# Two stacked blocks in split fp32: retention with its values first, rotary columns packed, and other places for the attention steps

## The chip, the cores and the metric

One core of one Trainium2 chip runs the kernel. The metric is the device time of one execution in microseconds (us). The kernel before takes 3192.93 us, the median of three runs (3192.46 to 3195.58).

## What is computed

Two networks of two layers each over 512 tokens of width 1024, one after the other, in float32.

Each layer of the first one ("mix") normalizes x, projects it and runs three attentions: differential attention (4 heads, "da"), latent attention (8 heads, "mla", two heads at a time) and sliding-window attention (8 heads, "sw", two at a time). Their gated outputs go through branch projections and an output projection; a gated embedding ("ple") follows. In latent attention a score is a 64-wide product plus a 32-wide rotary one:

```python
s = (jnp.einsum('bqhd,bkhd->bhqk', qn, kn)
     + jnp.einsum('bqhr,bkr->bhqk', qr, kr)) * scale
```

The second network has retention in its first layer: 4 heads with queries and keys 256 wide and values 512 wide, scores times a decay, no softmax, and then a normalization of the 512 outputs of a head to mean 0 and variance 1 (`mu`, `var`), times a gate. Its second layer has attention over three dilations (128, 512 and 2048 tokens), 16 heads, computed for two heads at a time in eight rounds. A convolutional feed-forward block follows each of the two.

## The kernel before

**Products.** All activations lie transposed, features in the partitions and the 512 tokens along the free axis. A linear product is a stream of steps; one step is a 128x128 piece of a weight against 128x512 of the activations, in three matmuls (L668 to L670: weight high part times activation high part, times low part, weight low part times high part). Eight steps (a tile) give 128 output columns when the inner dimension is 1024. `open` (L641) makes a tile wait until the bank of PSUM that it writes has been evicted. The weights come as a stream of chunks of eight steps through a ring of three buffers: SP loads a chunk, ScalarE casts the high part (L1145), GpSimd subtracts the low part (L535), and the matmuls use it.

**Order.** Each engine has its own program, written out by hand, and they meet at semaphores. `ORDER` (L70) lists for each of the 12 heads or pairs of heads of a layer which tiles TensorE computes beside the head's attention: gates, branches and the projections of the next head. `cuts` (L98) divides this work of head n into 12 equal parts. TensorE's loop over the four blocks of 128 queries (L843 on) puts three places into each block: after the first part `scores` of the next block, after the second `turn` (the transposes of the probabilities, L803), after the third `values` (probabilities times values, L823). The other engines follow the same cuts: VectorE takes the maxima of the scores, waits for the sums of ScalarE's exponentials, divides, and evicts the tiles in between (`beside`, L1885).

**Latent rotary columns.** The key's 32 rotary columns are projected twice, straight (`kr`, 8 steps) and with their halves swapped (`ks`, 8 steps), each with unused columns between; VectorE multiplies one with the cosine, one with the sine and adds (L1849 to L1856). The query's are `qr` and `qs`, 2 steps each, for each of the four pairs. The score uses 32 partitions of the result (L782). In head n = 3 the order is `kr`, `row_da`, `row_kv`, `ks`, and then `mv`, the values' step, which waits until the latent operand of `row_kv` is made (six operations of VectorE for the two rows: L1810, L1548, L1550 and L1825, L1548, L1550).

**Retention** (TensorE L913, ScalarE L1396, VectorE L2044). For each head: two tiles of queries, two of keys, four of values and four of the gate. VectorE evicts and rotates queries and keys (L2061 to L2074), evicts each value tile to `ret_vf` (L2081), TensorE turns it (L930); scores (L946), decay (L2087), scores times values (L959), copies (L1414). The mean over the 512 outputs is a product of the copies with a matrix of ones (L966), subtracted from them on VectorE (L2102); the squares of the differences go through a second one (L973), then a square root on ScalarE (L1156), a reciprocal of 128x512 on VectorE (L1563), and the finish: times gain and inverse, times the gate, split into high and low part (L2110, L2114, L1548, L1550), four times. After the finish VectorE comes to the next head's queries.

**Dilated attention.** Each round (`pair`, L1069) computes beside its four blocks the nine tiles of the next round: 5 steps, scores of the next block (L1007, L1014), 4 steps, the transposes (L1028, L1031), 9 steps, the sums (L1045 and at the end L1052). The last round has only the output projection beside it; there VectorE makes the low parts of that projection's operand (L2185) between the blocks.

## Time and profile before

| | |
|---|---|
| median of three runs | 3192.93 us |
| the profiled execution | 3191.41 us, its span 3189.6 us |
| TensorE busy | 3051.5 us, 96% of the span |
| VectorE busy | 1849.3 us, 58% |
| GpSimd / ScalarE busy | 1125.8 us, 35% / 1050.2 us, 33% |
| mean granted clock of TensorE | 0.981 |
| weights and inputs read | 257.56 MB, 83 GB/s over the span |

The span runs from the first to the last instruction of the profiled execution. A matmul's busy time is modelled and overlaps with the next one's, so the cost of a matmul is read from start to start. The idle time before a row stands in square brackets, with what ended it.

### The profile page before, as it was taken

What the parts mean: (1) busy time and instruction counts of PE and PEld (TensorE: products, weight loads), DVE (VectorE), ACT (ScalarE), POOL (GpSimd) and SP (SyncE); (2) the same over time, 40 slices, a digit from 0 to 9 for tenths busy, and PEclk for the clock granted to TensorE, in tenths of its full rate; (3) what the DMA queues carried; (4) which work ended last, traced back from release to release, by engine and by line L of the source; (5) the groups of instructions that cost most, each with busy time, mean ns of one, the idle gap of its engine ahead of it and who ended that gap; (6) DMA issues with size and microseconds to landing.
All of it is one profiled execution on the core that took longest, in us unless ns stands there. A gap on an engine that the chain in (4) does not pass through costs nothing.

```text
span 3189.6 us, 38922 instructions
## 1 busy us (share of the span) xinstructions
PE 3051.5 (96%) x15380; PEld 2389.9 (75%) x15380; DVE 1849.3 (58%) x3020; ACT 1050.2 (33%) x1848; POOL 1125.8 (35%) x472
## 2 busy tenths in 40 slices
PE   8999999999999999899999999998999999989998
PEld 6777768777777777767767878887777777778886
DVE  4766555465665554635543388822766666578832
ACT  4433342344333432422222232223333333332221
POOL 3332334333322333323332434443433333234442
PEclk9999999999999999999999999999999999999999
DMA  5222222222222222222121323331322222223232
GB/s 184 80 80 67 67 73 94 78 99 67 80 67 67 73 86 86 77 83 78 60 72 54 99 73 100 99 99 53 110 79 75 76 76 74 67 67 105 93 99 73
DMA packets 78761, 262.25 MB, mean 82 GB/s; under 512 B 10778, under 2 KB 13466, under 8 KB 78580
## 3 DMA queue, kind: packets, MB, share of 16 engines
q1 hardware_dynamic: 78004, 257.66, 25.2%
q8 instruction: 123, 2.02, 0.3%
q10 hardware_dynamic: 576, 2.10, 0.2%
q14 instruction: 58, 0.48, 0.0%
HBM read 257.56 MB, written 6.09 MB: 83 GB/s over the span
## 4 chain that ended last, share of the span: by engine, by line
PE 84%; DVE 11%; ACT 2%; issue 1%; DMA 1%; POOL 0%; SPq 0%; ACTq 0%; DVEq 0%
PE bank L668 25%; PE bank L670 23%; PE bank L669 23%; PE bank L776 2%; PE bank L823 2%; PE bank L803 1%; PE bank L959 1%; DVE x_res L1715 1%; PE bank L782 1%; DMA bias_copies<-bias_vectors 1%; PE bank L1007 1%; PE bank L1045 1%; ACT w_hi L1145 0%; POOL w_lo L535 0%; PE bank L946 0%
## 5 line engine op out<-in xcount | busy, mean ns | idle before, releaser
L535 POOL TENSOR_TENSOR w_lo<-w_raw,w_hi 128x1024 fp32r<-128x1024 f32 x462 | 1121.9, 2430 | 2009.0 <-ACT w_hi L1145 2009.0
L668 PE MATMUL bank<-h_hi,w_hi 128*128 128x512 f32 x2800 | 1146.0, 409 | 62.2 <-DVE h_lo L1703 20.4
L670 PE MATMUL bank<-h_hi,w_lo 128*128 128x512 f32 x2800 | 1102.4, 394 | 0.0
L669 PE MATMUL bank<-h_lo,w_hi 128*128 128x512 f32 x2800 | 1102.0, 394 | 0.0
L1145 ACT CAST w_hi<-w_raw 128x1024 fp32r<-128x1024 f32 x462 | 483.2, 1048 | 1273.7 <-PE bank L670 1254.5
L668 PEld LDWEIGHTS bank<-h_hi,w_hi 128*128 128x128 f32 x2800 | 532.9, 190 | 228.2 <-issue 88.2
L670 PEld LDWEIGHTS bank<-h_hi,w_lo 128*128 128x128 f32 x2800 | 531.6, 190 | 116.9
L669 PEld LDWEIGHTS bank<-h_lo,w_hi 128*128 128x128 f32 x2800 | 533.6, 191 | 101.1 <-issue 1.9
L1984 DVE TENSOR_SCALAR m<-bank,gains 128x512 f32<-128x512 f32 x48 | 36.0, 751 | 326.6 <-ACT ta L1344 202.6
L1277 ACT ACTIVATE probs<-probs,small_columns 128x128 f32<-128x128 f32 (+2 forms) x192 | 101.8, 530 | 217.5 <-DVE small_columns L1758 213.4
L670 PE MATMUL bank<-f_hi,w_lo 128*128 128x512 f32 x352 | 136.9, 389 | 0.0
L668 PE MATMUL bank<-f_hi,w_hi 128*128 128x512 f32 x352 | 136.9, 389 | 0.0
L669 PE MATMUL bank<-f_lo,w_hi 128*128 128x512 f32 x352 | 136.9, 389 | 0.0
L2147 DVE TENSOR_TENSOR tc<-ta,dil_sin 128x512 f32<-128x512 f32 x48 | 119.5, 2489 | 1.6
L1753 DVE CUSTOM_DVE_ANT_0 probs<-bank,bias 128x256 f32<-128x256 f32 (+3 forms) x128 | 56.3, 440 | 81.2 <-PE bank L776 77.5
L2040 DVE TENSOR_TENSOR ta<-ta,gelu 128x512 f32<-128x512 f32 x44 | 82.6, 1877 | 33.6 <-ACT gelu L1394 33.6
L2031 DVE SCALAR_TENSOR_TENSOR conv_out<-conv_in,gains,conv_out 128x512 f32<-128x512 f32 x44 | 93.7, 2130 | 1.6
L1287 ACT COPY pt<-bank 128x256 f32<-128x256 f32 (+3 forms) x160 | 55.5, 387 | 74.2 <-PE bank L803 73.6
L668 PE MATMUL bank<-zo_hi,w_hi 128*128 128x512 f32 x192 | 76.6, 399 | 0.0
L668 PEld LDWEIGHTS bank<-f_hi,w_hi 128*128 128x128 f32 x352 | 66.1, 188 | 13.8
L670 PEld LDWEIGHTS bank<-f_hi,w_lo 128*128 128x128 f32 x352 | 66.1, 188 | 13.8
L669 PEld LDWEIGHTS bank<-f_lo,w_hi 128*128 128x128 f32 x352 | 66.1, 188 | 13.5
(283 smaller groups left out, 3754.1 us busy)
## 6 DMA issues: line engine op xcount, KB each, us to landing
w_raw<-in_w SPq DMA_DIRECT2D x462, 512.0 KB, 3.5
bias_copies<-bias_vectors SPq DMA_DIRECT2D x1, 2560.0 KB
x_res<-in_x_t ACTq DMA_DIRECT2D x4, 512.0 KB, 8.0
bias<-bias_copies SPq DMA_DIRECT2D x8, 256.0 KB, 3.4
bias<-bias_copies SPq DMA_DIRECT2D x16, 128.0 KB, 2.4
out_x<-x_res SPq DMA_DIRECT2D x8, 256.0 KB, 2.0
bias_copies<-bias_vectors SPq DMA_DIRECT2D x1, 1280.0 KB
ple_raw<-in_p_t SPq DMA_DIRECT2D x2, 512.0 KB, 4.3
```

Of the source, the lines that this page charges most:

```text
L535: pool.tensor_tensor(WL[slot][:], RAW[slot][:], WH[slot][:].bitcast(F32), ALU.subtract).then_inc(sems["lo_done"], 1)
L668: pe.matmul(banks[bank][:], WH[slot][:, w], hi[:, k, :], start=start, stop=False)
L669: pe.matmul(banks[bank][:], WH[slot][:, w], lo[:, k, :], start=False, stop=False)
L670: pe.matmul(banks[bank][:], WL[slot][:, w], hi[:, k, :], start=False, stop=stop).then_inc(sems["kt_done"], 1)
L776: ins = pe.matmul(banks[S0 + m][:, 0:blocks * P], AQ[r, q], keys[r, kk], start=True, stop=(kind != "mla"))
L823: ins = pe.matmul(banks[OUTB][r, i * P:(i + 1) * P], v, p[:, b * P:(b + 1) * P], start=(b == 0), stop=(b == blocks - 1))
L1145: act.copy(WH[slot][:], RAW[slot][:]).then_inc(sems["hi_done"], t.one("hi_done"))
L1277: act.activation(s, s, ACT.Exp, bias=sm(NM + u), accum_out=sm(DEN + u)).then_inc(sems["exped"], t.one("exped"))
L1753: dve.tensor_tensor_reduce(SS[i % 2][m][:, 0:w], banks[S0 + m][:, 0:w], bias, 1.0, LOWEST, ALU.add, ALU.max, sm(MX + u)).then_inc(sems["dv ...
L2031: dve.scalar_tensor_tensor(CO[j][:], GE[j][:, 1:SEQ + 1], conv(x, 1), CO[j][:], ALU.mult, ALU.add).then_inc(sems["dve_step"], t.one("dve_s ...
L2040: dve.tensor_tensor(TA[:], TA[:], GL[j][:], ALU.mult).then_inc(sems["dve_step"], t.one("dve_step"))
L2147: dve.tensor_tensor(TC[:], TA[:], DS[:], ALU.mult).then_inc(sems["dve_step"], t.one("dve_step"))
```

## The change

**Latent rotary columns.** `qr` now holds straight and swapped columns side by side, 64 partitions for a head, and one table holds cosine in 32 of them and signed sine in the others; `qs` is gone. The key has the same layout, and a 128x128 product with a 0/1 matrix (`fold_kr`) adds its two halves into both; `ks` is gone. The score takes 64 partitions. One more constant of 64 KB is loaded at the start.

**Places.** `cuts` makes 9 parts. A block has two places: scores of the next block together with the values of the block before, and the turn. The last values of a head stand with the first scores of the next.

```diff
 KINDS = ["da"] * 4 + ["mla"] * 4 + ["sw"] * 4
-LATENT = [("mv", 1), ("qn", 2), ("qr", 2), ("qs", 2), ("kn", 1)]
+LATENT = [("mv", 1), ("qn", 2), ("qr", 2), ("kn", 1)]
+         [("cv", 8), ("sum_da", 0), ("sum_kv", 0), ("ck", 8), ("turn_cv", 0), ("kr", 8), ("row_da", 0), ("row_kv", 0), ("fold_kr", 0)] + LATENT + [("z", 8)],
          [("g0", 8), ("sum_da", 0), ("g1", 8), ("row_da", 0), ("z", 8)] + LATENT + BRANCH,
...
-    share = (total - first) / 12
-    return [upto(n, round(first + share * (p + 1))) for p in range(12)]
+    share = (total - first) / 9
+    return [upto(n, round(first + share * (p + 1))) for p in range(9)]
...
+    straight = p % HEAD < ROPE
+    c["columns"] = np.stack([inv[p % HALF], np.where(straight, 1.0, sign), np.where(straight, math.pi / 2, 0.0)], 1).astype(f)
+            elif name == "fold_kr":
+                bank = self.rotate(3)
+                t.up("k_scaled")
+                pe.wait_ge(sems["k_scaled"], t.at("k_scaled"))
+                pe.matmul(banks[bank][:], FOLD[:], KR[:], start=True, stop=True).then_inc(sems["folded"], t.one("folded"))
...
-                r = slice(64 * m, 64 * m + ROPE)
+                r = slice(64 * m, 64 * m + 64)
...
-            fill(n, at_[3 * i])
+            fill(n, at_[2 * i])
             if i + 1 < QT:
                 scores(n, i + 1)
-            fill(n, at_[3 * i + 1])
+            if i:
+                values(n, i - 1)
+            fill(n, at_[2 * i + 1])
             turn(n, i)
-            fill(n, at_[3 * i + 2])
-            if i + 1 == QT and n + 1 < 12:
-                scores(n + 1, 0)
-            values(n, i)
+        fill(n, at_[8])
+        if n + 1 < 12:
+            scores(n + 1, 0)
+        values(n, QT - 1)
...
-        elif name in ("kr", "ks"):
-            dve.tensor_tensor(TB[:], bank, RSTD[:], ALU.mult).then_inc(sems["evicted"], 1)
+        elif name == "kr":
+            dve.tensor_tensor(KR[:], bank, RSTD[:], ALU.mult).then_inc(sems["evicted"], 1)
             self.settle()
-            if name == "kr":
-                dve.tensor_tensor(KR[:], TB[:], COS[:], ALU.mult).then_inc(sems["dve_step"], t.one("dve_step"))
-            else:
-                dve.tensor_tensor(TB[:], TB[:], SIN[:], ALU.mult).then_inc(sems["dve_step"], t.one("dve_step"))
-                dve.wait_ge(sems["dve_step"], t.at("dve_step"))
-                dve.tensor_tensor(KR[:], KR[:], TB[:], ALU.add).then_inc(sems["dve_step"], t.one("dve_step"))
...
-        elif name == "qs":
-            dve.scalar_tensor_tensor(TB[:], bank, scale["mla"], SIN[:], ALU.mult, ALU.mult).then_inc(sems["evicted"], 1)
-            self.settle()
-            dve.tensor_tensor(AR[:], AR[:], TB[:], ALU.add).then_inc(sems["dve_step"], t.one("dve_step"))
-            dve.wait_ge(sems["dve_step"], t.at("dve_step"))
...
+            elif name == "fold_kr":
+                t.up("folded")
+                dve.wait_ge(sems["folded"], t.at("folded"))
+                self.tiles += 1
+                dve.tensor_copy(KR[:], banks[self.rot % 3][:]).then_inc(sems["evicted"], 1)
+                self.settle()
...
-        kr = [tiles(wi, np.concatenate([o["bkr"] + r, gap, o["bkr"] + r, gap])) for r in (rope, swap)]
+        kr = tiles(wi, np.concatenate([o["bkr"] + r for r in (rope, swap)] * 2))
+            if name == "qr":
+return tiles(qb, np.concatenate([96 * x + HEAD + r for x in h for r in (rope, swap)]))
```

**Retention.** The four value tiles come first, then queries, keys, gate. The value tiles, turned, are centred over their 512 columns before they are used (the mean by the accumulator of a copy on ScalarE, the subtraction on VectorE), which makes the outputs' mean 0. Their squares are added on VectorE and summed with four matmuls of one column (`all_squares`, as elsewhere in the kernel); the square root and the reciprocal work on 128x4, and the row is spread by four transposes. The finish of a head stands between the evictions of the next head's values, and the last head's before the output projection. The gate's second tile is divided around the scores.

```diff
-    def body(h):
+    for h in range(RET_HEADS):
+        v = self.tiles
         if h == 0:
             self.together([self.open(b) for b in range(3)], HH, HL, KT, KT)
+            self.open(3)
+            half(3, 0)
             self.all_squares(OUTB, SQ2)
-            self.whole(self.open(3))
+            half(3, KT // 2)
             self.spread(OUTB)
+            turn(v)
         else:
             for j in range(4):
                 self.whole(self.open(j))
+                if j == 0:
+                    self.spread(RS0)
+                else:
+                    turn(v + j - 1)
+        self.whole(self.open(0))
+        turn(v + (1 if h == 0 else 3))
+        for j in range(1, 4):
             self.whole(self.open(j))
-            if j:
-                turn(self.tiles - 2)
+            if h == 0 and j < 3:
+                turn(v + j + 1)
+        self.whole(self.open(0))
+        self.open(1)
+        half(1, 0)
         t.up("rotated", 4)
         pe.wait_ge(sems["rotated"], t.at("rotated"))
         for kt in range(QT):
...
                 ins = pe.matmul(banks[RS0 + kt % 2][:, 0:n], RK[:, c, kt * P:(kt + 1) * P],
                                 RQ[:, c, kt * P:SEQ], start=(c == 0), stop=(c == 1))
             ins.then_inc(sems["s_ready"], t.one("s_ready"))
-            if kt == 1:
-                turn(self.tiles - 1)
+        half(1, KT // 2)
         t.up("decayed", 2)
         pe.wait_ge(sems["decayed"], t.at("decayed"))
+        t.up("centred", QT)
...
-            t.up("y_copied")
+            t.up("ret_squared")
             if e >= 2:
-                pe.wait_ge(sems["y_copied"], t.at("y_copied", -2))
+                pe.wait_ge(sems["ret_squared"], t.at("ret_squared", -2))
...
-        self.whole(self.open(0))
-        pe.wait_ge(sems["y_copied"], t.at("y_copied"))
-        for e in range(4):
-            ins = pe.matmul(banks[RS0][:], ONES[:], RY[:, e, :], start=(e == 0), stop=(e == 3))
-        ins.then_inc(sems["small"], t.one("small"))
-        self.whole(self.open(1))
         self.whole(self.open(2))
-        for e in range(4):
-            t.up("ret_squared")
-            pe.wait_ge(sems["ret_squared"], t.at("ret_squared"))
-            ins = pe.matmul(banks[RS0 + 1][:], ONES[:], RSQ[:, e, :], start=(e == 0), stop=(e == 3))
-        ins.then_inc(sems["summed"], t.one("summed"))
         self.whole(self.open(3))
-    t.turns(RET_HEADS, body)
+        self.all_squares(RS0, RSQ)
     self.rot = 0
...
+            if j == (3 if h == 0 else 1):
+                for kt in range(QT):
+                    act.wait_ge(sems["v_token"], t.at("v_token"))
+                    if kt:
+                        act.wait_ge(sems["v_mean"], t.at("v_mean"))
+                    act.activation(RSQ[:, 1, :], RVT[:, kt, :], ACT.Copy, scale=-1.0 / RET_V,
+                                   accum_out=sm(MX + kt)).then_inc(sems["v_mean"], t.one("v_mean"))
...
+            if e == 3:
+                act.wait_ge(sems["sq_added"], t.at("sq_added", 1))
+            act.activation(RSQ[:, (0, 1, 2, 1)[e], :], banks[RTURN + e % 2][:], ACT.Square).then_inc(sems["ret_squared"], t.one("ret_squared"))
...
+    def value(h, j):
+
+        if h == 0 and j < 3:
+            self.tiles += 1
+            self.n += 3 * KT if j == 0 else 0
+            dve.wait_ge(sems["kt_done"], self.n)
+        else:
+            self.tile(KT)
+        if t.k.get("v_turned", 0):
+            dve.wait_ge(sems["v_turned"], t.at("v_turned"))
+        t.up("v_turned")
+        dve.tensor_tensor(RVF2[:], banks[j][:], RSTD[:], ALU.mult).then_inc(sems["evicted"], 1)
+
+    def centre():
+        for kt in range(QT):
+            t.up("v_mean")
+            dve.wait_ge(sems["v_mean"], t.at("v_mean"))
+            dve.tensor_scalar(RVT[:, kt, :], RVT[:, kt, :], sm(MX + kt), None, ALU.add).then_inc(sems["centred"], t.one("centred"))
...
+    def finish(h, e):
+
+        if e == 0:
+            t.up("rstd_spread")
+            dve.wait_ge(sems["rstd_spread"], t.at("rstd_spread"))
+            t.up("gate", 4)
+            dve.wait_ge(sems["gate"], t.at("gate"))
...
+            value(h, j)
+            if h:
+                finish(h - 1, j)
+        rotary(RQ, 0)
+        rotary(RK, 2)
+        centre()
...
+        for e in range(4):
+            t.up("ret_squared")
+            if e:
+                dve.wait_ge(sems["ret_squared"], t.at("ret_squared"))
+                dve.tensor_tensor(RSQ[:, 0, :], RSQ[:, 0, :], RSQ[:, (0, 1, 2, 1)[e], :], ALU.add).then_inc(sems[name], t.one(name))
...
+        inverses(RS0, RET_V)
+    for e in range(4):
+        finish(RET_HEADS - 1, e)
```

**Dilated attention.** The sums of block i stand beside the scores of block i+2, between 9 and 9 steps; in the last round VectorE makes the low parts ahead of each block's maxima and divisions.

```diff
+        if not more:
+            turn_values(self.v)
+            for i in range(QT):
+                if i < 3:
+                    s_pair(par, i + 1)
+                t_unit(i, 0)
+                t_unit(i, 1)
+                out_steps(i)
+                pv_pair(par, i)
+            return
         for i in range(QT):
             at_ = 18 * i
-            if more:
-                steps(nxt, at_, at_ + 5)
+            first, last = at_ + (6 if i == 3 else 9), at_ + (11 if i == 3 else 18)
+            steps(nxt, at_, first)
             if i == 0:
                 turn_values(self.v)
-            elif more and i == 3:
+            elif i == 3:
                 turn_values(self.tiles - 2)
             if i < 3:
                 s_pair(par, i + 1)
-            if more:
-                steps(nxt, at_ + 5, at_ + 9)
+            if i:
+                pv_pair(par, i - 1)
+            if i == 1:
+                turn_values(self.tiles - 2)
+            steps(nxt, first, last)
             t_unit(i, 0)
             t_unit(i, 1)
-            if more:
-                if i == 1:
-                    turn_values(self.tiles - 2)
-                steps(nxt, at_ + 9, at_ + 18)
-                if i == 3:
-                    self.v = self.tiles - 1
-                    t.up("rotated", 6)
-                    pe.wait_ge(sems["rotated"], t.at("rotated"))
-                    s_pair(nxt, 0)
-            else:
-                out_steps(i)
-            pv_pair(par, i)
+        steps(nxt, last, 72)
+        self.v = self.tiles - 1
+        t.up("rotated", 6)
+        pe.wait_ge(sems["rotated"], t.at("rotated"))
+        s_pair(nxt, 0)
+        pv_pair(par, QT - 1)
...
+        else:
+            out_lo(0)
+            for i in range(1, QT):
+                u1(i)
+                out_lo(i)
+                u2(i)
```

## Rows read from the trace of the kernel before

**Rows 1.** The page: span, TensorE's busy time, and the chain of waits by engine.

```profile
span 3189.6 us, 38922 instructions
PE 3051.5 (96%) x15380; PEld 2389.9 (75%) x15380; DVE 1849.3 (58%) x3020; ACT 1050.2 (33%) x1848; POOL 1125.8 (35%) x472
...
PE 84%; DVE 11%; ACT 2%; issue 1%; DMA 1%; POOL 0%; SPq 0%; ACTq 0%; DVEq 0%
```

**Rows 2.** TensorE's waits by releaser: us in total, times, longest us.

```profile
PE bank L668 <- DVE ta L2061: 14.4, 4, 5.5
...
PE bank L930 <- DVE ret_vf L2081: 11.5, 4, 5.2
...
PE bank L803 <- DVE probs L1775: 5.6, 12, 1.6
...
PE bank L668 <- DVE h_lo L2185: 5.0, 3, 1.7
```

**Rows 3.** Timeline of TensorE, two steps in a row: start us, us, instruction.

```profile
1556.20 0.39 PE L668 MATMUL bank<-h_hi,w_hi 128*128 128x512 f32 x1
...
1556.88 0.39 PE L668 MATMUL bank<-h_hi,w_hi 128*128 128x512 f32 x1
```

**Rows 4.** Timeline of TensorE, head 1 of retention to the next one's scores.

```profile
1507.33 3.17 PE L946 MATMUL bank<-ret_q,ret_k 128*128 128x512 f32 x8
...
1526.86 3.60 PE L966 MATMUL bank<-ret_y,ones 128*128 128x512 f32 x8
1529.89 0.79 PE L668 MATMUL bank<-h_hi,w_hi 128*128 128x512 f32 x1
1530.52 0.40 PE L669 MATMUL bank<-h_lo,w_hi 128*128 128x512 f32 x1
...
1603.09 0.60 PE L930 MATMUL bank<-ident,ret_vf 128*128 128x128 f32 x4
1603.53 1.02 PE L946 MATMUL bank<-ret_q,ret_k 128*128 128x512 f32 x2
```

**Rows 5.** Timeline of TensorE, the sum of squares of one column before retention.

```profile
1371.24 0.95 PE L697 MATMUL bank<-ones,sq 128*128 128x1 f32 x8
1372.05 0.49 PE L668 MATMUL bank<-h_hi,w_hi 128*128 128x512 f32 x1
```

**Rows 6.** Timeline of TensorE, a wait of head 2 and the matmuls after it.

```profile
1577.48 0.80 PE L668 MATMUL bank<-h_hi,w_hi 128*128 128x512 f32 x1 [5.48 <-DVE ta L2061]
...
1578.50 0.63 PE L670 MATMUL bank<-h_hi,w_lo 128*128 128x512 f32 x1
1578.93 0.63 PE L668 MATMUL bank<-h_hi,w_hi 128*128 128x512 f32 x1
...
1581.92 0.40 PE L669 MATMUL bank<-h_lo,w_hi 128*128 128x512 f32 x1
```

**Rows 7.** Timeline of VectorE and GpSimd in the same head.

```profile
1553.36 3.35 DVE L1563 RECIPROCAL rstd<-var 128x512 f32<-128x512 f32 x1 [7.84 <-ACT var L1156]
...
1578.19 0.69 DVE L2064 TENSOR_TENSOR ret_q<-ta,ret_cos 128x512 f32<-128x512 f32 x1
...
1586.89 2.77 DVE L2072 TENSOR_TENSOR tc<-ta,ret_sin 128x512 f32<-128x512 f32 x1
...
1586.49 2.62 POOL L535 TENSOR_TENSOR w_lo<-w_raw,w_hi 128x1024 fp32r<-128x1024 f32 x1 [10.80 <-ACT w_hi L1145]
```

**Rows 8.** Timeline of TensorE, one place for values in a latent head.

```profile
257.49 0.40 PE L670 MATMUL bank<-h_hi,w_lo 128*128 128x512 f32 x1
257.81 0.66 PE L823 MATMUL bank<-pt,att_vt 128*64 128x128 f32 x8
258.40 0.50 PE L668 MATMUL bank<-h_hi,w_hi 128*128 128x512 f32 x1
258.74 0.39 PE L669 MATMUL bank<-h_lo,w_hi 128*128 128x512 f32 x1
```

**Rows 9.** Timeline of head n = 3 of layer 0: VectorE, then TensorE.

```profile
172.52 0.69 DVE L1849 TENSOR_TENSOR tb<-bank,rstd 128x512 f32<-128x512 f32 x1 [1.57 <-PE bank L670]
...
178.49 0.69 DVE L1550 TENSOR_TENSOR kvn_lo<-lat_q,kvn_hi 128x512 fp32r<-128x512 f32 x1
...
187.23 0.50 PE L668 MATMUL bank<-qn_hi,w_hi 128*128 128x512 f32 x1 [2.17 <-DVE var L1860]
```

More of the change, by code:

```diff
@@ L676, in whole, with together @@
                         self.kt(bank, hi, lo, k, k == 0, k == KT - 1)
-                def together(self, opened, hi, lo, nk, fresh):
+                def together(self, opened, hi, lo, nk, fresh, spread=None):
                     for k in range(nk):
+                        if k == 1 and spread is not None:
+                            self.spread(spread)
                         if k >= nk - fresh:
@@ L871, in linear @@
                         t.up("operand", nk)
-                        self.together([self.rotate() for _ in range(first)], hi, lo, nk, fresh)
+                        self.together([self.rotate() for _ in range(first)], hi, lo, nk, fresh, RS0 if name == "ret" else None)
                     for _ in range(first, KT):
@@ L1245, in beside @@
                             self.n += nk > 0
-                            if nk and k == nk - 1 or name.startswith(("sum", "row")):
+                            if nk and k == nk - 1 or name.startswith(("sum", "row", "fold")):
                                 self.tiles += 1
@@ L1427, in body @@
                             act.activation(RP[:, e, :], RP[:, e, :], ACT.Silu).then_inc(sems["gate"], t.one("gate"))
-                    t.turns(RET_HEADS, body)
+                        silu(0)
+                        silu(1)
+                        self.past(1, KT)
+                        silu(2)
+                        self.past(1, KT)
+                        silu(3)
+                        root()
                 def dilated(self):
@@ L1471, in pair @@
+                            hi(self.n)
+                            return
+                        to(9)
                         self.v_out(DVT[par][:, 2], DAUX)
-                        if not more:
-                            out_hi(0)
                         e_pair(1)
-                        to(9)
+                        to(18)
                         c_pair(0)
-                        to(23)
-                        if not more:
-                            out_hi(1)
+                        to(27)
```

285 lines of the change are left out of this document (127 added, 158 removed).

## The prediction, made before the change was run

> **What bounds the kernel now.** I read the page first, then TensorE's waits, then its timeline. TensorE is busy for 3051.5 of 3189.6 us and carries 84% of the chain of waits [rows 1]. So a change pays if it takes instructions, waits or breaks out of TensorE's stream; what VectorE and ScalarE save counts only where TensorE waits for them. The waits are few, and two of the largest lie in retention: 14.4 us for the eviction of the queries (`ta`) and 11.5 us for the first value tiles [rows 2]. A step of the stream (three matmuls) takes 0.68 us from start to start, 0.227 us a matmul [rows 3].
>
> A wait costs more than itself. Head 2 of retention waits 5.48 us, and then the matmuls start 0.43 us apart, TensorE's clock of 1.2 GHz instead of 2.4; from 1577.48 to 1581.92 ten of them take 4.44 us instead of 2.27, so 2.2 us more [rows 6].
>
> A break costs too. At a place for values, the last matmul before it takes 0.32 us until the next start and the first one after it 0.34 us, instead of 0.23 [rows 8]: 0.2 us a place beside the work done in it.
>
> **Retention, per head.** The two products with ones go. The first stands from 1526.86 to 1529.89, 3.03 us, and the first matmul after it takes 0.63 instead of 0.23 us [rows 4]; the second is of the same form. So 2 x 3.43 = 6.9 us a head, 27.4 us in four. In their place come a one-column sum of 0.81 us [rows 5] and a spread of four transposes, by a turn 0.44 us [rows 4], each with a break of 0.2: 1.65 us a head, +6.6 us in all. Turns that stood inside the score block now stand apart, and the gate tile is divided between scores and sums: three more breaks a head, 3 x 0.2 x 4 = +2.4 us.
>
> The waits. Now VectorE reaches the finish only after the square root and a reciprocal of 3.35 us, and the next head's queries only after the finish; at 1553.36 it begins the reciprocal, and at 1577.48 TensorE starts again [rows 6, 7]. The change puts the values there, which want one eviction each (0.7 us), with a quarter of the finish behind each. That quarter is four operations of 0.7 us or less, about 2.7 us, plus 2.1 us where one meets GpSimd: a product of two tiles in SBUF took 2.77 instead of 0.69 us while GpSimd's subtraction ran [rows 7]. 0.7 + 2.7 + 2.1 = 5.5 us lies within a tile of 8 x 0.68 = 5.4 us and the turn of 0.44. The queries come when the finish is over. I let all 25.9 us [rows 2] go, and with them about 2.2 us at half the clock in each head: -34.7 us.
>
> What is late next. The four copies with accumulators on ScalarE (each taken at 0.8 us, an estimate from the 0.69 us of an operation of this size [rows 7] and the reading of its sum) delay its weight casts by 3.2 us; it is busy for 33% of the span and the ring holds two more chunks, of 5.4 us each: nothing. After the last key tile VectorE must evict it (0.7), make six rotary products and sums (4.3), centre four tiles (2.9) and decay the first score block (0.7), with two meetings with GpSimd (4.2): 12.8 us. TensorE has 12 steps (8.2 us) and two score blocks (about 3 us) before it needs that block: it waits some 1.5 us, and once without the meetings not at all. I put 1.2 us x 4, and 2 us in head 0, where the first turn now follows directly on the copy of the inverse and the eviction of a value: +6.8 us. Behind the waiting VectorE instruction only score blocks 1 to 3 are queued. The squares and adds lie beside sums and gate tiles. The square root is behind two casts and silus, but the next value tile covers it; before the output projection only one step of three tiles covers it, under 1 us once. Sum: -27.4 + 6.6 + 2.4 - 34.7 + 6.8 = **-46 us**. Bounds: -57 with no new waits, -20 if each head keeps a wait like that of rows 6.
>
> **Rotary columns.** `ks` is 8 steps, `qs` 4 x 2, in two layers: 32 steps x 0.68 = -21.8 us. The score's 64 instead of 32 partitions change nothing for TensorE, since the columns that stream are the same; VectorE's saved operations stand beside other work. The four chunks of weights less free SP, ScalarE and GpSimd, which do not bound.
>
> But `ks` was cover. In n = 3 VectorE begins to evict `kr` at 172.52 and has the values' operand at 179.18 [rows 9]. Until now 8 steps of `ks` lay between. Now TensorE is through the two spreads near 173.2, waits for the scaled key until 173.9 (0.7 us), folds (0.8 us, a quarter of 3.03 [rows 4]) and waits at `mv` from 174.8 to about 179.2, 4.4 us. That is nearer to the wait of 5.48 [rows 6] than to that of 2.17 us [rows 9], so I add 2.2 us at half clock. Behind `mv` lie the turn and the latent steps of the whole pair. The old wait of 2.17 us for VectorE's copy of the values [rows 9] goes, since the copy comes right after the step. 0.7 + 0.8 + 4.4 + 2.2 - 2.2 = 5.9, two layers +11.8 us. Bounds +3 (VectorE quicker without GpSimd, no half clock) and +16. The extra constant comes while SP waits for the bias vectors: nothing. Sum: **-10 us**.
>
> **Places.** A head had 11 breaks for its attention (three in each of blocks 0 to 2, two in the last) and gets 9: 2 x 12 x 2 = 48 fewer at 0.2 us, **-9.6 us**. No row shows scores and values side by side in the middle of a head; a break could save 0.1 to 0.25 us, so -5 to -12. From scores to their turn there were four parts of 3.3 steps and are three of 4.4, the same; for the first block of a head it grows from 6.7 to 8.9 steps, 1.5 us, and the 12 waits for probabilities (5.6 us [rows 2], at most 1.6 each) mostly go: **-4 us**, between 0 and -7.
>
> **Dilated attention.** Three breaks fewer in seven rounds, 21 x 0.2 = **-4.2 us**. In the last round the 5.0 us for the low parts [rows 2] go when these come before maxima and divisions, but the probabilities come later by them (1.3 us a block): **-4 us**, between 0 and -7.
>
> **Sum.** -46 - 10 - 9.6 - 4 - 4.2 - 4 = -78 us. The profiled execution took 3191.4 us, so 3113.6 us; the median of the runs is 1.5 us above it: **3115 us**.
>
> **Rivals.**
> - *The waits in retention come back as others.* If the centring and GpSimd's meetings hold the decay, or a quarter of the finish runs over its tile, TensorE stops by 3 to 5 us in each head and then runs at half clock: 4 x (4.5 + 2.2) = 27 us less gain, 3142 us. For it: VectorE operations of 2.77 us [rows 7]. Against it: 12.8 us against 11.2, a wait too short for that. The Trainium skill ("TensorE: Matmul & The Clock Gate", section on the oscillation in real kernels) says that a stall which returns in each round lets the clock fall each time; by that rule this rival's 2.2 us would be paid in every head, and the trace agrees, as rows 6 show.
> - *Slower than before.* Values at the front of a block instead of its end hold up the stream in each of 96 blocks: the turn waits for probabilities, which VectorE makes only after the evictions of its longer part. It decides from 0.8 us a block (78 / 96); at 1 us the time is 3115 + 96 = 3211 us. For it: there are waits of up to 1.6 us at the turn [rows 2]. Against: they are 12, and the distance doesn't shrink.
> - *More than summed.* VectorE is ahead everywhere, `mv` waits under 2 us, half clock goes with it, breaks give 0.25 us: 78 + 7 + 9 + 3 = 97 us, 3096 us.
> - *The breaks give nothing*, because the switch from scores to values costs what a return to the stream did: 14 us less, 3129 us.
>
> **Chances.** The forecast (3105 to 3125) 0.55; waits in retention 0.13; more than summed 0.15; no gain by breaks 0.13; slower 0.03; that a product isn't dropped as said, 0.01. The range goes from 3096 to 3137 us: it takes in three of these cases and the milder half of the waits in retention. A measurement of this kernel can tell about 0.2% (6 us) from no change. Faster 0.96, the same 0.01, slower 0.03.
>
> **What would show it.** In the profile after: no rows of a 128x512 product with ones but the dilated one; TensorE's waits for `ta` and `ret_vf` under 3 us in all; a head of retention in about 84 to 85 us instead of 96.2 (1507.33 to 1603.53 [rows 4]); a wait of 3 to 5 us at `mv` twice, with matmuls 0.43 us apart behind it; fewer than three waits at the turn. It is wrong if TensorE waits for `ret_p` or `ret_vt` by more than 3 us a head, if the turns wait in many blocks, or if TensorE's busy time falls by less than 45 us.

## The result, and the profile after

The changed kernel takes **3072.97 us** (median of 4 runs, 3071.18 to 3075.39), beside 3194.26 us of the kernel before in the same comparison (4 runs). The ratio is 0.9621, 95% interval 0.9609 to 0.9633: 121 us less, where 78 were forecast, and the time lies below the range. A second comparison gave 3072.29 us and 0.9625 (0.9612 to 0.9639). The profiled execution took 3071.18 us around a span of 3069.4 us, 120.2 less than before.

The page of the kernel after (span; busy time; chain of waits by engine), against [rows 1]:

```profile
span 3069.4 us, 38687 instructions
PE 2972.8 (97%) x15272; PEld 2362.1 (77%) x15272; DVE 1851.8 (60%) x3007; ACT 1060.2 (35%) x1875; POOL 1119.1 (36%) x468
...
PE 89%; DVE 6%; ACT 2%; DMA 1%; issue 1%; POOL 0%; SPq 0%; ACTq 0%; DVEq 0%
```

TensorE's busy time falls by 78.7 us and the span by 120.2: the other 41.5 us were idle time. TensorE's waits in the kernel after (us in total, times, longest), against [rows 2]:

```profile
PE bank L671 <- issue: 8.1, 2, 4.0
...
PE bank L977 <- DVE ret_p L2162: 1.7, 4, 0.4
PE bank L671 <- DVE h_lo L2244: 1.6, 1, 1.6
...
PE bank L934 <- DVE ret_vf L2105: 1.5, 1, 1.5
PE bank L747 <- DVE k_rope L1897: 1.5, 2, 0.7
...
PE bank L813 <- DVE probs L1821: 1.3, 4, 0.7
```

The waits for the queries (14.4 us) are gone and those for value tiles fell from 11.5 to 1.5; at the turn 5.6 became 1.3 and 0.9; the last dilated round waits 1.6 instead of 5.0. New are two waits at the product on the latent values (8.1 us, given as "issue", longest 4.0) and two at the fold. Most of this was forecast. A wait that the prediction never named went too; TensorE's waits in the kernel **before** hold this row:

```profile
PE bank L668 <- DVE tb L1877: 12.1, 2, 6.1
```

It is nowhere in the kernel after. With matmuls of the same name as marks in both traces, the span divides like this:

| stretch | before, us | after, us | difference |
|---|---|---|---|
| heads 0 to 10, layer 0 / 1 | 424.8 / 423.3 | 408.2 / 407.3 | -16.6 / -16.0 |
| head 11 to the output projection, layer 0 / 1 | 104.2 / 104.2 | 96.0 / 96.4 | -8.2 / -7.8 |
| output projection, layer 0 / 1 | 49.4 / 49.8 | 47.0 / 47.0 | -2.5 / -2.8 |
| after layer 1's projection, with all of retention | 454.4 | 398.4 | -56.0 |
| dilated attention and second feed-forward | 966.5 | 954.2 | -12.3 |
| all the rest | 613.0 | 615.0 | +2.0 |

### The profile page after: what moved, and what is told of

Read it like the earlier page. It is cut to its first block, busy times and chain, and to the rows that moved or that the text cites. A ratio compares the mean times of both kernels' runs of the same rounds, so it can differ in the third digit from the quotient of the medians.

```text
span 3069.4 us, 38687 instructions
## 1 busy us (share of the span) xinstructions
PE 2972.8 (97%) x15272; PEld 2362.1 (77%) x15272; DVE 1851.8 (60%) x3007; ACT 1060.2 (35%) x1875; POOL 1119.1 (36%) x468
## 4 chain that ended last, share of the span: by engine, by line
PE 89%; DVE 6%; ACT 2%; DMA 1%; issue 1%; POOL 0%; SPq 0%; ACTq 0%; DVEq 0%
PE bank L671 26%; PE bank L673 25%; PE bank L672 25%; PE bank L786 2%; PE bank L833 2%; PE bank L813 1%; PE bank L991 1%; DVE x_res L1761 1%; PE bank L702 1%; DMA bias_copies<-bias_vectors 1%; PE bank L1027 1%; PE bank L792 1%; PE bank L1065 1%; DVE ret_vt L2111 0%; DMA w_raw<-in_w 0%
## 5 line engine op out<-in xcount | busy, mean ns | idle before, releaser
L671 PE MATMUL bank<-h_hi,w_hi 128*128 128x512 f32 x2784 | 1124.7, 404 | 43.5 <-DVE h_lo L1749 20.4
```

The costliest lines, as they stand in the source:

```text
L671: pe.matmul(banks[bank][:], WH[slot][:, w], hi[:, k, :], start=start, stop=False)
```

## The experiments

Six kernels took one part of the change alone, three put one thing back into the kernel after, two tried another order in it, and one ran it again. The kernel before, run beside them, had a median of 3193.17 us for the first four below (retention, bank, 64 rows, packed columns), 3192.68 for the places, the dilated part, the bank put back and the latent row first, 3194.54 for the finish in one lump, the two products and the other order, and 3193.41 for the kernel after run again. Gains on the kernel before are differences of medians to these; differences to the kernel after go by its 3072.97 us. Behind the median stand the ratio to the kernel before and its 95% interval; a width of 0.0025 is 8 us.

**Retention alone**, on the kernel before (what the diff does in `retention`; its core):

```
-                        for e in range(4):
-                            ins = pe.matmul(banks[RS0][:], ONES[:], RY[:, e, :], start=(e == 0), stop=(e == 3))
...
+                        self.all_squares(RS0, RSQ)
...
+                            value(h, j)
+                            if h:
+                                finish(h - 1, j)
```

> The kernel before with the retention part of the change alone. Theory: retention gives what the two traces differ by in that stretch, 56 us (454.4 us before and 398.4 us after, from the first step of the second embedding gate to the output projection), so 3138 us. Rival, the recorded prediction: 46 us, 3148 us, and the 10 us more came with another part.

3139.32 us (ratio 0.9828, 0.9813 to 0.9843): -53.9 us. The theory holds (55.9 us less in that stretch of its trace); the prediction's -46 is too small.

**The bank of the output projection alone**, on the kernel before:

```
-        LINEAR_BANK = {"post": sum(name != "turn_cv" for order in ORDER for name, _ in order), "ret": 0,
+        LINEAR_BANK = {"post": 3 + sum(name != "turn_cv" for order in ORDER for name, _ in order), "ret": 0,
...
+                    if name == "post":
+                        self.rot += 3
```

The second edit moves TensorE's own count of the rotation on by the same 3 before that projection.

> The kernel before, with nothing but the output projection of each mix layer beginning at bank 3 of the rotation instead of bank 0. Theory: the wait of 6.1 us there, twice, and the matmuls at half clock after it (2.3 us each) are a collision of the first tile of the projection with the bank of the last branch tile, which VectorE hasn't evicted; both go, 17 us less, 3177 us. Rival: the wait is for VectorE's operands of the projection, and stays: within 2 us of before.

3176.69 us (0.9948, 0.9935 to 0.9960): **-16.5 us**, with no work taken out. TensorE at this place in the kernel before (start us, us, instruction):

```profile
563.53 0.39 PE L670 MATMUL bank<-zo_hi,w_lo 128*128 128x512 f32 x1
569.99 0.79 PE L668 MATMUL bank<-y_hi,w_hi 128*128 128x512 f32 x1 [6.07 <-DVE tb L1877]
570.58 0.63 PE L669 MATMUL bank<-y_lo,w_hi 128*128 128x512 f32 x1
```

and its busy time and granted clock in the ten matmuls from there on (start to end, us, busy and count, granted clock, DMA share, GB/s):

```profile
569.99:574.40 4.41, 4.41 (x10) 0.50 0.04 16
```

In the kernel after the projection follows without a gap:

```profile
545.46 0.39 PE L673 MATMUL bank<-zo_hi,w_lo 128*128 128x512 f32 x1
545.68 0.39 PE L671 MATMUL bank<-y_hi,w_hi 128*128 128x512 f32 x1
```

What happens here: whatever the attention's layer puts into a bank beside its own products (tiles, column sums, spread rows) goes round three banks (0 to 2), the projection's tiles go round seven, and they begin at the number of the former mod 7. The kernel before had 112 of them: the last one, a branch tile, stood in bank 0 (111 mod 3), and the projection began in bank 0 too (112 mod 7), so it had to wait for the eviction of the tile just made. The packed columns take out five (`ks` and four `qs`) and put one in (`fold_kr`), which leaves 108: the last one is in bank 2, and the projection begins in bank 3. The Trainium skill ("Perfetto Trace Analysis", section "Matmuls") says that independent groups should go through different banks, so that the evacuation of one overlaps the next one's matmuls; by that rule the wait is what a wrong bank costs, and the traces agree, with 6.07 us and half the clock behind it.

**64 rows in the rotary score alone**, on the kernel before: the same numbers, rows of zeros with them.

```
-                                r = slice(64 * m, 64 * m + ROPE)
+                                r = slice(64 * m, 64 * m + 64)
```

> The kernel before, with the rotary score product over 64 partitions instead of 32 (the 32 more are zeros). Theory: a pair of products over the same 64 rows as the first pair saves a switch of 0.2 us that the 32-row pair costs, 32 blocks, 6.4 us less, 3188 us. Rival: the width does nothing, and the 0.2 us a block come from elsewhere: 3194 us.

3185.5 us (0.9975, 0.9965 to 0.9985): **-7.7 us**. One block of two key blocks, kernel before:

```profile
199.86 0.70 PE L776 MATMUL bank<-att_k,att_q 64*128 64x256 f32 x4
200.49 0.70 PE L782 MATMUL bank<-k_rope,att_qr 32*128 32x256 f32 x4
201.12 0.50 PE L668 MATMUL bank<-h_hi,w_hi 128*128 128x512 f32 x1
```

and with 64 rows:

```profile
201.86 0.70 PE L776 MATMUL bank<-att_k,att_q 64*128 64x256 f32 x4
202.40 0.60 PE L782 MATMUL bank<-k_rope,att_qr 64*128 64x256 f32 x4
202.92 0.50 PE L668 MATMUL bank<-h_hi,w_hi 128*128 128x512 f32 x1
```

1.26 us become 1.06, in 32 blocks. The single matmuls of these rows show where: the first rotary score starts 0.31 us after the score before it with 32 rows and 0.21 with 64, and so does the second after the first; the step back to the stream takes 0.31 us in both kernels. The Trainium skill ("TensorEngine Tiling (Array Packing)", section "Key Properties") says that changing the tiling mode, not just the tile, drains TensorE. The traces agree: one change of the tile's form costs about 0.2 us here, 0.1 in the step before it and 0.1 in the step behind it, and 64-row scores in a row pay none between them. By the trace heads 4 to 7 give 0.75 to 0.81 us each, 6.2 in all; the other 1.5 us lie in stages without an edit.

**The packed columns alone**, on the kernel before (`ks` gone, `qs` gone, `fold_kr` in):

```
-LATENT = [("mv", 1), ("qn", 2), ("qr", 2), ("qs", 2), ("kn", 1)]
+LATENT = [("mv", 1), ("qn", 2), ("qr", 2), ("kn", 1)]
...
-                                r = slice(64 * m, 64 * m + ROPE)
+                                r = slice(64 * m, 64 * m + 64)
```

> The kernel before with the packed and folded rotary columns alone. Theory: 32 steps less (21.8 us), the bank at which the projection begins moves by itself from 0 to 3 (17 us), 64 rows (6.4 us), less the waits at the fold and at mv (2 x 4.0 + 1.5 us), the fold (1.6 us) and half clock, plus the old wait of 2.2 us twice: about 37 us less, 3157 us. Rival, the recorded prediction: 10 us less, 3184 us.

3158.84 us (0.9892, 0.9878 to 0.9905): -34.3 us. Less the bank's 16.5 and the rows' 7.7 that it contains, 10.1 us are left, beside the -10 of the prediction. Each of the three has an interval of 3 to 4 us to either side, so that they alone would not show it; the trace does better: up to head 10 the two layers are 17.1 us shorter, and less the rows' 6.2 that is 10.9.

**Two places per block alone**, on the kernel before (the values of block i-1 behind the scores of block i+1, at the first of two cuts, in place of a third cut of their own):

```
-                            values(n, i)
...
+                            if i:
+                                values(n, i - 1)
```

> The kernel before with two places per block in place of three in the one-pair attention, and nothing else (the bank of the projection stays where it was). The prediction's terms: 48 breaks at 0.2 us and the waits at the turn, -13.6 us together, so about 3180 us. Theory after reading the two traces: the places pay only where a break is really saved. Heads 0 to 3 of a layer give 0 to 1 us (head 0: the wait behind its first block), heads 4 to 7 some 0.4 us each, heads 8 to 11 0.9 to 1.5 us each, and the last stretch of each layer 2 us: about -19 us, 3174 us. Rival: the longer distance is worth nothing without the packed columns, -10 us or less.

3175.11 us (0.9947, 0.9934 to 0.9959): -17.6 us. By its trace head 0 of layer 0 gives 2.5, heads 1 and 2 nothing, heads 4 to 7 some 0.5 us each, heads 8 to 10 0.9 to 1.5, the two last stretches 1.9 each; head 3 takes 1.6 us more in one layer and 1.6 less in the other. Why the first give nothing shows in head 1; kernel before, the values between two tiles:

```profile
92.91 0.39 PE L670 MATMUL bank<-h_hi,w_lo 128*128 128x512 f32 x1
93.14 0.60 PE L823 MATMUL bank<-pt,att_vt 128*128 128x128 f32 x4
93.50 0.48 PE L668 MATMUL bank<-h_hi,w_hi 128*128 128x512 f32 x1
```

and kernel after, scores and values together:

```profile
92.42 1.13 PE L786 MATMUL bank<-att_k,att_q 64*128 64x512 f32 x4
93.48 0.71 PE L833 MATMUL bank<-pt,att_vt 128*128 128x128 f32 x4
93.94 0.47 PE L671 MATMUL bank<-h_hi,w_hi 128*128 128x512 f32 x1
```

A value product of these heads is a tile of 128*128, as in the stream: its step starts 0.23 us after the one before it, not 0.32 as in [rows 8], where the tile is 128*64. There was no change of mode to save; 0.36 us of values became 0.46 behind the 64-row scores.

**The dilated part alone**, on the kernel before (two cuts in a block in place of three, and the last round's order by hand):

```
-                            if more:
-                                steps(nxt, at_, at_ + 5)
+                            first, last = at_ + (6 if i == 3 else 9), at_ + (11 if i == 3 else 18)
+                            steps(nxt, at_, first)
```

> The kernel before with the dilated part of the change alone: column sums beside scores two blocks on, low parts ahead of maxima in the last round. The prediction's terms give -8.2 us (-4.2 for 21 breaks, -4 for the last round). Theory after reading the two traces: -12.3 us between the feed-forward and the end, 3181 us, with the wait for the low parts of the last round going from 5.0 to 1.6 us; rival: part of the 12.3 us came from the place of the banks after the packed layers, and this kernel shows -8 us.

3182.87 us (11 runs; 0.9973, 0.9964 to 0.9982): -9.8 us, between the two. In its trace the stretch is 12.2 shorter: 1.0 at one wait ahead of the first round, 4.2 in seven rounds (0.6 each, as three breaks of 0.2 say), 3.9 in the last round (33.15 us became 29.24), and 3.1 behind two waits that stay as they are: after 2.71 us for the last low part of the output projection's operand, and after 1.84 us for weights in the second feed-forward, the kernel before runs seven or eight matmuls at half clock and this one none (1.5 and 1.6 us).

These 3.1 us can't be put down to the edit. The wait of 2.71 us stands in all fourteen profiles of this case: seven run at half clock behind it (the kernel before, retention, bank, packed columns, bank put back, latent row first, other order) and seven at full clock. And in this very run heads 2 and 3 of layer 0, whose instructions are those of the kernel before, take 1.57 and 1.61 us more; in head 2 this is the granted clock, here and then in the kernel before:

```profile
121.30:124.70 3.40, 3.40 (x12) 0.51 0.28 70
```
```profile
121.30:124.70 3.40, 3.40 (x19) 1.00 0.28 84
```

**The bank put back**, on the kernel after: `LINEAR_BANK["post"]` four higher, the rotation moved on by 4.

> The kernel after with one thing put back: the output projection of each layer begins again at bank 0, which the last value tile has just used, as in the kernel before. Theory (the start of that projection was a wait for a bank, which the change removed by having fewer tiles ahead of it): TensorE waits about 6 us for VectorE at the start of both projections and then runs at half clock, +16.5 us, so about 3089.5 us. Rival (the last block's work is shorter in the kernel after, so that the bank is free in time): under +5 us.

3096.94 us (0.9701, 0.9688 to 0.9714): +24.0. TensorE waits again:

```profile
PE bank L671 <- DVE tb L1914: 12.5, 2, 6.2
```

The two stretches before the projection and the projections grow by 16.5 us in the trace, as the theory said; 7.1 more stand in later stages that are the same in both kernels, 1.6 of them at half clock behind the wait of 2.71 us. So the mechanism is shown both ways, and its size is 16.5 us; the rest is not shown to be its doing.

**All of the finish behind the first value tile**, on the kernel after:

```
-                            if h:
-                                finish(h - 1, j)
+                            if h and j == 0:
+                                for e in range(4):
+                                    finish(h - 1, e)
```

> The kernel after, but in retention VectorE does all four quarters of a head's finish behind the first value tile of the next head, in place of one quarter behind each. Theory (a quarter fits under a tile of 5.4 us, four don't): VectorE is 8 to 15 us at the finish, TensorE gets past tiles 1 to 3 on free banks and stops once in each of heads 1 to 3 for an eviction, for 3 to 8 us, with half clock behind it, +15 to +30 us in all, 3088 to 3103 us. Rival (VectorE catches up under the four key and query tiles, so that where its finish stands does not matter and the gain is that of the products alone): within 3 us of the kernel after.

3100.40 us (0.9708, 0.9694 to 0.9723): +27.4. TensorE's waits in its retention:

```profile
PE bank L934 <- DVE ret_vf L2105: 19.7, 4, 6.1
```

and one of them, with the granted clock of the wait and of the matmuls behind it:

```profile
1410.66 1.12 PE L934 MATMUL bank<-ident,ret_vf 128*128 128x128 f32 x4 [6.07 <-DVE ret_vf L2105]
```
```profile
1404.60:1410.60 6.00, 0.00 (x0) 0.91 0.31 100
1410.66:1415.50 4.84, 4.84 (x14) 0.50 0.06 24
```

Three heads stop for 6 us and pay half the clock each time: 25.4 us in retention. That is what the rival "the waits come back" (27 us) describes; what brings it about here is the place of three quarters of the finish. The rule of the Trainium skill ("TensorE: Matmul & The Clock Gate", section on the oscillation in real kernels) on stalls that return in each round, which the prediction weighed, is borne out by the trace: each of the three heads pays anew.

**Two products with ones a head put in again**, on the kernel after, in the last gate tiles; nobody reads them:

```
+                        for e in range(4):
+                            pe.matmul(banks[RS0 + 1][:], ONES[:], RVT[:, e, :], start=(e == 0), stop=(e == 3))
```

> The kernel after with two products of 128x512 with ones (four matmuls each) put into the last gate tiles of each head of retention, read by nobody. It prices the two products that the change took out. The prediction's term: 2 x 3.43 us a head, +27.4 us, 3100 us. Theory after reading the two traces: 3.03 us each and some 0.2 to 0.4 us of break, +26 to +27 us. Rival (part of such a product lies beside a wait of TensorE that is there anyway): under +20 us.

3103.76 us (0.9716, 0.9700 to 0.9732): +30.8; by the traces +27.6 in retention, 6.9 us a head (and 3.1 in head 0 of layer 0, where nothing was edited):

```profile
1380.71 3.60 PE L997 MATMUL bank<-ret_vt,ones 128*128 128x512 f32 x8
1383.75 0.79 PE L671 MATMUL bank<-h_hi,w_hi 128*128 128x512 f32 x1
1384.38 0.40 PE L672 MATMUL bank<-h_lo,w_hi 128*128 128x512 f32 x1
```

The product takes 3.04 us, and the first matmul behind it 0.63 in place of 0.23, as [rows 4] had it. The prediction's price of 3.43 us a product holds.

**The latent row first**, on the kernel after (`sum_kv`, `row_kv` ahead of `sum_da`, `row_da`; the product waits for `made + 4` instead of `made + 5`):

> The kernel after with the row of the latent value before the row of the query/key pair, and the product on the latent values waiting for the latent row alone. Theory (the 4 us wait at that product is VectorE's work on two rows in sequence, about 2 us each): the wait falls from 4.0 to about 2 us in both layers and the half clock behind it goes or shortens, -4 to -8 us, 3065 to 3069 us. Rival: VectorE has to finish both anyway because the next step reads the other row: the wait moves to the fold or to the steps behind it, within 1 us of the kernel after.

3074.48 us (0.9630, 0.9617 to 0.9643): no gain. The waits fell as expected,

```profile
PE bank L671 <- issue: 4.2, 2, 2.1
```

and head 3 of the two layers is 4.9 us shorter; +1.0 in head 0, +1.6 ahead of the first feed-forward and +2.7 in the dilated stretch took it back.

**Latent row before the key tile, pair's row after the latent steps**, on the kernel after:

```
-         [("cv", 8), ("sum_da", 0), ("sum_kv", 0), ("ck", 8), ("turn_cv", 0), ("kr", 8), ("row_da", 0), ("row_kv", 0), ("fold_kr", 0)] + LATENT + [("z", 8)],
+         [("cv", 8), ("sum_kv", 0), ("sum_da", 0), ("ck", 8), ("turn_cv", 0), ("row_kv", 0), ("kr", 8), ("fold_kr", 0)] + LATENT + [("row_da", 0), ("z", 8)],
...
-                                        pe.wait_ge(sems["made"], made + 5)
+                                        pe.wait_ge(sems["made"], made + 4)
```

> The kernel after with another order in n = 3 of each layer: the row of the latent value is spread before the rotary key tile, the row of the query/key pair after the latent steps, and the product on the latent values waits for the latent row alone. Theory (the 4.0 us at that product are VectorE's work on rows after the key tile, which the key tile itself could cover): the wait goes from 4.0 to under 1 us in each layer, the matmuls behind it run at full clock, and at most 1.5 us stands before the fold in place of 0.7: -8 to -12 us, 3061 to 3065 us. Rival (VectorE is as late again for probabilities, or the time comes back as waits in the next blocks, as the latent row put first alone brought no measurable gain): within 3 us of the kernel after.

3069.46 us (3067.39 to 3070.60; 0.9611, 0.9597 to 0.9625). At the place it does all that was asked: the fold waits 1.6 us, the product on the values follows it, and the clock is full (0.23 us from start to start):

```profile
175.07 1.10 PE L747 MATMUL bank<-k_rope,fold_sb 128*128 128x512 f32 x2 [1.60 <-DVE k_rope L1897]
175.60 0.80 PE L671 MATMUL bank<-kvn_hi,w_hi 128*128 128x512 f32 x1
176.24 0.40 PE L672 MATMUL bank<-kvn_lo,w_hi 128*128 128x512 f32 x1
176.47 0.39 PE L673 MATMUL bank<-kvn_hi,w_lo 128*128 128x512 f32 x1
```

Head 3 is 5.65 and 5.50 us shorter. But in the same trace 10 us come back: 1.0 up to the end of head 0, 1.9 in the output projections and behind the first, 1.3 with retention, 1.6 in the first feed-forward, 4.5 in the dilated stretch (0.4 less at the end). Of the last, 3.2 us are the clock again: behind the waits of 2.71 and 1.9 us that both kernels have, the kernel after runs at full clock and this one starts seven or eight matmuls 0.43 us apart. The first of the two waits, kernel after and then this one:

```profile
2645.59 0.50 PE L671 MATMUL bank<-h_hi,w_hi 128*128 128x512 f32 x1 [2.71 <-DVE h_lo L2007]
2645.93 0.40 PE L672 MATMUL bank<-h_lo,w_hi 128*128 128x512 f32 x1
```
```profile
2641.65 0.78 PE L671 MATMUL bank<-h_hi,w_hi 128*128 128x512 f32 x1 [2.71 <-DVE h_lo L2007]
2642.23 0.63 PE L672 MATMUL bank<-h_lo,w_hi 128*128 128x512 f32 x1
```

The other 1.3 us stand ahead of the dilated part, where VectorE's work on the low parts meets GpSimd's subtractions. Kernel after, one operation of each:

```profile
2138.45 1.15 DVE L2184 SCALAR_TENSOR_TENSOR h_lo<-x_res,gains,h_hi 128x512 fp32r<-128x512 f32 x1
```
```profile
2138.60 3.21 POOL L538 TENSOR_TENSOR w_lo<-w_raw,w_hi 128x1024 fp32r<-128x1024 f32 x1
```

and this one:

```profile
2133.15 3.23 DVE L2184 SCALAR_TENSOR_TENSOR h_lo<-x_res,gains,h_hi 128x512 fp32r<-128x512 f32 x1
```
```profile
2133.11 2.41 POOL L538 TENSOR_TENSOR w_lo<-w_raw,w_hi 128x1024 fp32r<-128x1024 f32 x1
```

What differs is which begins first. VectorE's operation begins 0.15 us ahead of GpSimd's in the kernel after, and GpSimd's takes 3.21 us instead of 2.4. Here it begins 0.04 us behind GpSimd's, takes 3.23 us instead of 1.15 and ends 0.86 us after it. TensorE then waits 1.9 instead of 0.6 us for these low parts.

**The kernel after, again:**

> The kernel after, unchanged, a second time, to set the kernel with the rows in another order against: that one gains 11 us in the two blocks of attention it changes and gives 9 us back in stages that it does not touch (1.1 and 0.4 us before and 1.3 in retention, 1.6 before the feed-forward, 4.5 in the dilated part). Theory (what came back is how weights, VectorE and GpSimd happen to meet in the later stages, which differs between executions of one and the same program): this profile shows steps of 1.5 us against the first one at the same places (the operand before the first feed-forward tile, the second tile after it), a span 2 to 6 us above 3069.4, and the median of its runs is 3072 to 3076 us, so that the other order is 3 to 6 us faster. Rival (the later stages are late because the attention ends earlier): span and later stages as in the first profile within 0.5 us.

3072.29 us (3070.56 to 3079.02), span 3068.8, and every stretch from head 1 on within 0.4 us of the first profile. The profile goes against my theory, and it is what the rival said it would be. But it doesn't settle the matter. Both profiles are of the fastest execution of their comparison (3071.18 and 3070.56 us), and the other executions of this one kernel reach 3079.02, at a mean granted clock of 0.984 where the fastest have 0.986. So that the 10 us belong to the kernel with the other order isn't shown, nor that its later stages are late *because* the attention ends earlier: with the bank put back the attention ends later, and there too 1.6 us come at the wait of 2.71 us. What decides the clock behind such a wait stays open. The other order is 3 us faster than the kernel after by the medians, but the intervals of the two ratios overlap, so it isn't shown to be faster.

## Why the prediction was right or wrong

| part | forecast, us | alone on the chip, us |
|---|---|---|
| retention | -46 | -53.9 |
| rotary columns | -10 | -34.3 |
| places and waits at the turn | -13.6 | -17.6 |
| dilated attention | -8.2 | -9.8 |
| sum | -78 | -115.6 (together -121.3) |

(The whole has 5.7 us over its parts. The interval of each part is 3 to 5 us wide to either side, and stages without any edit gave or took up to 7.1 us in the runs above, so nothing is to be read into them.)

**The rotary columns: two steps failed, and they make more than half of the miss.** The first is an omission. "Rotary columns" counted the steps that go and not what their going does to the turn of the banks: a wait of 6.07 us and half clock behind it in each layer, 16.5 us, put at nothing. The wait it removes was the third largest in the list that [rows 2] are from, and I took only the rows that the diff's own lines explained. The second is the sentence "The score's 64 instead of 32 partitions change nothing for TensorE, since the columns that stream are the same": the streaming is the same, the changes of mode aren't (7.7 us). What was left of the part came out at 10.1 for 10 (10.9 by the trace), with its inner terms: the wait at `mv` 4.04 (4.4 forecast), at the fold 0.73 (0.7), and half clock behind it (the second fence: busy time and granted clock of that stretch):

```profile
178.74 0.76 PE L671 MATMUL bank<-kvn_hi,w_hi 128*128 128x512 f32 x1 [4.04 <-issue]
179.31 0.63 PE L672 MATMUL bank<-kvn_lo,w_hi 128*128 128x512 f32 x1
```
```profile
178.74:183.30 4.56, 4.56 (x12) 0.50 0.30 118
```

**Retention: right mechanism, one term mis-sized.** A head takes 82.28 us (scores at 1358.35 and 1440.63), not 84 to 85. The products cost what was said, the old waits and their half clock went whole. The failed term is "new waits, +6.8": measured are 0.4 us at `ret_p` in each head and 1.5 once at the turn. The kernel before already had the four waits of 0.4 (1.5 us in all), so only 1.7 us are new. VectorE's centring, its longest new work there, met little of GpSimd:

```profile
1439.90 3.66 DVE L2111 TENSOR_SCALAR ret_vt<-ret_vt,small_columns 128x512 f32<-128x512 f32 x4
```

Two meetings of 2.1 us each had been put into that sum. The three more breaks a head (+2.4 us) hardly cost anything either: the turns and the column sums are tiles of 128*128, and the whole of the stream between them in a head is 0.7 us over 288 x 0.2275 us. A value's eviction with its quarter of the finish took VectorE 5.3 us at the first tile and 4.8 at the next (5.5 forecast), inside the tile.

**Places: the total near, the division wrong.** "48 breaks at 0.2" is 0.4 us a head. It fails in heads 0 to 3, where a value product changes no mode and gives nothing. In heads 4 to 7 it holds (0.5 us a head): each of the two merged places saves one change of the tile's form. The waits for probabilities with their late restarts, and the last stretches, gave more than the -4.

**Dilated:** the rounds gave 0.6 us each and the last round 3.9, as said. What the trace has beyond that is 1.0 us at a wait ahead of the rounds, which the prediction doesn't name, and 3.1 us of clock behind two unchanged waits, which stands in the -121.3 of the whole change too and isn't shown to be its gain.

**The rivals.** "More than summed" was nearest in sign, but its reasons weren't the ones: `mv` did wait 4 us, and half clock came. "The breaks give nothing" is true of heads 0 to 3 alone. "The waits come back" didn't happen, and the kernel with the finish in one lump shows that it was the quarters that kept it away. The range was built from the bounds of the terms that I had; no bound covers a term that is missing, and the largest one was.

## What to carry to other kernels

Where the work rotates over a fixed number of banks, a change in the number of tiles changes who meets whom at the end of a stage: work out the count modulo the banks before and after, and give a reason for every wait in the list above a few us, not only for those on lines of the diff. Price a break by whether the tile's form changes on TensorE and not by its being a break. And a wait removed in one stage is worth what the whole kernel's time says: 11 us less in the blocks of one head gave 3 in the end. Before a few us in an unedited stage are given a reason, compare the granted clock behind its waits in both traces.

## What the runs showed of the hardware that was not expected

- A change between 128*128, 64*128, 32*128 and 128*64 tiles cost about 0.2 us in these streams, 0.1 in the step before it (0.32 instead of 0.23 us to the next start) and about 0.1 in the step behind it; between two tiles of the same form there was no such cost.
- After waits of 4.04 and 6.07 us the next 10 to 14 matmuls ran at a granted clock of 0.50, at 1.2 instead of 2.4 GHz. After 1.60 us in the kernel with the other order they stood 0.23 us apart. After one and the same wait of 2.71 us seven of fourteen profiles show half clock and seven full clock, at a difference of 1.5 us. Over a wait of 6 us itself the granted clock was 0.91 in the mean.
- The same VectorE operation took 1.15 us in one kernel and 1.14 in its second profile, where it began ahead of GpSimd's, and 3.23 in another, where GpSimd's had begun 0.04 us earlier; in the first case GpSimd's took 3.21 us instead of 2.4.
